# PEER routing in bf16, one gate piece on ScalarE, routings two and four blocks closer

## The chip, the cores and the metric

One core of one Trainium2 chip runs the whole program. The metric is device time in microseconds (us) of one execution. Before the change the median of 3 runs is 3424.29 us (3423.9 to 3427.24).

## What is computed

Two residual layers over 512 tokens of width 1024. Each has an attention mixture, and behind it a PEER layer (product-key experts), which is the stage that the change touches:

```python
def peer(xn, w_q, sub_keys, u, v):
    q = (xt @ w_q).reshape(T, PEER_HEADS, 2, PEER_HALF)
    s = jnp.einsum('thpc,hpnc->thpn', q, sub_keys).astype(jnp.float32)
    s1, i1 = lax.top_k(s[:, :, 0], PEER_TOPK)
    s2, i2 = lax.top_k(s[:, :, 1], PEER_TOPK)
    cand = (s1[..., :, None] + s2[..., None, :])...      # 8 heads x 256 sums
    cidx = (i1[..., :, None] * PEER_N_KEYS + i2[..., None, :])...
    top_s, top_j = lax.top_k(cand, PEER_TOPK)
    expert = jnp.take_along_axis(cidx, top_j, axis=-1)
    gate = jax.nn.softmax(top_s, axis=-1)
    # per token: out = sum over 128 experts of gate * gelu(x . u[expert]) * v[expert]
```

There are 16384 experts (128 x 128), and each token takes 8 heads x 16 of them.

## The kernel before

**Tiling.** The 512 tokens are four tiles of 128 (t = 0 to 3). Tile 0 is done sparsely: GpSimd fetches its experts' rows of u and v by indirect DMA (`fetch`), VectorE multiplies and sums them (`use_row`). Tiles 1 to 3 (384 tokens, `SD`) are done densely: TensorE multiplies them with all of u and all of v, and the hiddens are weighted by a gate matrix that is zero but for the chosen experts.

**Blocks.** `peer_stage` is written as one row of blocks n, and each engine has its own loop over them, in program order. Blocks 0 to 15 project the queries (`NQ`), 16 to 143 multiply with u (`FRONT` is 144), and the 128 behind them with v. A block of u is 24 matmuls of 384 columns into `h_ps` (`product`, L1884), since each fp32 operand is split into a high and a low part: ScalarE makes the high part two blocks ahead (`upper(n + 2)`, L1959, 128x1024), and VectorE or GpSimd the low one (`lower(n + 2)`, L2173 or L1850). ScalarE then takes the product through Gelu (`take`, L1973) and SyncE stores it.

**Routing.** For each tile t VectorE runs `route(t)` as a generator in pieces, one for each block from `route_step[t]` on: 18, 26, 61 and 96 (`LIST_END` is 18). The pieces are: sums of candidates and the upper eight (L2064, L2070), their places (L2074), the lower eight and the shifted scores (L2079 to L2084), arithmetic on the places (L2091 to L2104), then the translation of the places to key numbers. For each side s that is 16 `scalar_tensor_tensor` (L2110: is_equal with c, times key number c) into a table of 16 x 128 fp32, and one `tensor_reduce` over it (L2115). The last piece divides the gates (L2122) and signals `routed`. In the nine blocks of a routing (`ROUTE_PIECES`, `in_route`) GpSimd makes the low part of block n + 2 in VectorE's place, so VectorE's first own low part is that of block `route_step + 11`. VectorE also uses about nine fetched rows in ten blocks throughout (L2181).

**Turning and cutting.** At the end of block `route_step + 9` TensorE waits for `routed` and transposes both picks and the gates into `t_ps` (L1906 to L1908). At `route_step + 10` VectorE cuts the gates into three bf16 pieces (`cut_gates`, L2136 to L2144).

**Gate matrix.** From `route_step + 11` on, 16 batches of 8 tokens follow for each tile, 7 blocks for five batches (`hot_step`). For each, VectorE writes in bf16 `same` (L2160), `rows` (L2164) and three `cols`, one for each piece (L2168), all 128x1024. Two blocks later TensorE multiplies them in the middle of a block (`place_gates`, 24 matmuls, L1920), and ScalarE moves the result (`move_gates`, 2 x 128x512, L1995). Every fourth batch, SyncE stores 2 MB of gates. Four blocks behind the last batch (`WEIGH0`, block 134) SyncE loads the first hiddens and gates back (`load_w`, L1824 and L1825); the first weighings and high and low parts of the weights follow at `WEIGH0 + 3` to `WEIGH0 + 6`. They are needed at block 144.

## Time and profile before

| | |
|---|---|
| median of 3 runs | 3424.29 us |
| profiled execution | 3423.7 us |
| its span, first to last instruction | 3421.9 us |
| mean granted TensorE clock | 0.977 |
| TensorE matmul / VectorE / ScalarE / GpSimd busy | 95% / 78% / 41% / 32% |
| u phase of layer 0's PEER, with the queries | 336 to 1070 us |
| u phase of layer 1's PEER, with the queries | 2144 to 2879 us |

Each engine runs its own program in order and waits on semaphores. In the views below "x16" means that many instructions merged into one row, "[5.96 <-DVE ...]" means that the engine sat idle for 5.96 us until that instruction of VectorE (DVE) ended, and PE, ACT, POOL and SP are TensorE, ScalarE, GpSimd and SyncE. Layer 0's tiles are called p0r_..., layer 1's p1r_....

### The profile page before, as it was taken

How to read it: one execution, taken by the hardware profiler on the slowest of the kernel's cores; microseconds unless marked ns; L12 is line 12 of the kernel's file. 1: busy time of each engine (PE TensorE's matmuls, PEld its weight loads, DVE VectorE, ACT ScalarE, POOL GpSimd, SP SyncE). 2: the span in 40 equal slices, each digit the busy share in tenths (PEclk: the TensorE clock that was granted, in tenths of full speed). 3: DMA queues.
4: the chain of work that ended last, by engine and by line, in shares of the span. 5: the costliest groups of instructions: out<-in, count | busy, mean ns of one | idle time of the engine just before them, and what ended most of it. 6: DMA issues, size and time to landing. Idle time of an engine off the chain costs nothing. (4 is left out here: it accounts for less than half of the span.)

```text
span 3421.9 us, 49213 instructions
## 1 busy us (share of the span) xinstructions
PE 3255.3 (95%) x18534; PEld 2913.3 (85%) x18534; DVE 2667.6 (78%) x5415; ACT 1400.2 (41%) x2205; POOL 1098.5 (32%) x666
## 2 busy tenths in 40 slices
PE   7988999999999999998999997999999999999997
PEld 6866899999998888886978876899989998888886
DVE  4664799888976889885367875799898976888886
ACT  3333245544453333333345544235545453333332
POOL 1311363333422465550000001354242422455451
PEclk9998999999999999999999999999999999999999
DMA  4102358878889999994122212348778789999994
GB/s 164 62 7 89 127 163 288 297 268 294 274 310 352 406 392 402 387 397 144 71 80 69 75 44 81 130 138 293 288 268 282 271 313 350 409 398 394 392 396 178
DMA packets 324348, 833.65 MB, mean 244 GB/s; under 512 B 26000, under 2 KB 160656, under 8 KB 320016
## 3 DMA queue, kind: packets, MB, share of 16 engines
q1 hardware_dynamic: 250384, 562.04, 45.8%
q0 software_dynamic: 73728, 268.47, 21.3%
q8 instruction: 148, 2.42, 0.3%
q14 instruction: 88, 0.72, 0.1%
HBM read 721.30 MB, written 109.10 MB: 243 GB/s over the span
## 5 line engine op out<-in xcount | busy, mean ns | idle before, releaser
L1959 ACT ACTIVATE peer_hi<-peer_raw 128x1024 fp32r<-128x1024 f32 x540 | 570.7, 1057 | 648.8 <-PE p_bank L1933 501.1
L2173 DVE TENSOR_TENSOR peer_lo<-peer_raw,peer_hi 128x1024 fp32r<-128x1024 f32 x434 | 532.0, 1226 | 315.2 <-ACT peer_hi L1959 314.9
L1862 POOL DMA_INDIRECT p_grow<-in_u_rows,p_expert x256 | 331.2, 1294 | 750.1 <-DVE p_hid L2181 736.1
L1862 POOL DMA_INDIRECT p_grow<-in_v_rows,p_expert x256 | 425.1, 1660 | 372.4 <-DVE p_acc L2190 331.4
L1933 PE MATMUL p_bank<-peer_hi,p_w_hi 128*128 128x512 f32 x1536 | 473.1, 389 | 0.8 <-DVE peer_lo L2173 0.8
L1933 PE MATMUL p_bank<-peer_hi,p_w_lo 128*128 128x512 f32 x1536 | 473.0, 389 | 0.0
L1933 PE MATMUL p_bank<-peer_lo,p_w_hi 128*128 128x512 f32 x1536 | 472.8, 389 | 0.0
L1884 PE MATMUL p0r_h_ps<-peer_x_hi,peer_hi 128*128 128x384 f32 (+1 forms) x1152 | 400.8, 348 | 9.7 <-ACT p_h_sb L1973 5.8
L1884 PE MATMUL p1r_h_ps<-peer_x_hi,peer_hi 128*128 128x384 f32 (+1 forms) x1152 | 401.1, 348 | 9.3 <-ACT p_h_sb L1973 5.6
L1884 PE MATMUL p1r_h_ps<-peer_x_hi,peer_lo 128*128 128x384 f32 (+1 forms) x1152 | 394.9, 343 | 0.0
L1884 PE MATMUL p1r_h_ps<-peer_x_lo,peer_hi 128*128 128x384 f32 (+1 forms) x1152 | 394.9, 343 | 0.0
L1884 PE MATMUL p0r_h_ps<-peer_x_hi,peer_lo 128*128 128x384 f32 (+1 forms) x1152 | 394.8, 343 | 0.0
L1884 PE MATMUL p0r_h_ps<-peer_x_lo,peer_hi 128*128 128x384 f32 (+1 forms) x1152 | 394.7, 343 | 0.0
L1850 POOL TENSOR_TENSOR peer_lo<-peer_raw,peer_hi 128x1024 fp32r<-128x1024 f32 x106 | 267.9, 2529 | 372.7 <-ACT peer_hi L1959 372.1
L1933 PEld LDWEIGHTS p_bank<-peer_hi,p_w_hi 128*128 128x128 f32 x1536 | 288.1, 188 | 61.4 <-DVE peer_lo L2173 1.7
L1933 PEld LDWEIGHTS p_bank<-peer_hi,p_w_lo 128*128 128x128 f32 x1536 | 288.3, 188 | 60.0
L1933 PEld LDWEIGHTS p_bank<-peer_lo,p_w_hi 128*128 128x128 f32 x1536 | 288.3, 188 | 59.8
L2181 DVE CUSTOM_DVE_ANT_0 p_grow<-p_grow,p_xrow 128x1024 f32<-128x1024 f32 x256 | 318.2, 1248 | 0.8
L2190 DVE SCALAR_TENSOR_TENSOR p_acc<-p_grow,p_w,p_acc 128x1024 f32<-128x1024 f32 x252 | 317.6, 1279 | 0.0
L1884 PEld LDWEIGHTS p0r_h_ps<-peer_x_hi,peer_hi 128*128 128x128 f32 x1152 | 218.5, 190 | 15.3 <-issue 9.1
L1884 PEld LDWEIGHTS p1r_h_ps<-peer_x_hi,peer_hi 128*128 128x128 f32 x1152 | 218.6, 190 | 15.0 <-issue 8.6
L1884 PEld LDWEIGHTS p1r_h_ps<-peer_x_lo,peer_hi 128*128 128x128 f32 x1152 | 218.3, 189 | 5.2
(365 smaller groups left out, 5589.2 us busy)
## 6 DMA issues: line engine op xcount, KB each, us to landing
peer_raw<-in_u SPq DMA_DIRECT2D x256, 512.0 KB, 5.0
peer_raw<-in_v SPq DMA_DIRECT2D x256, 512.0 KB, 9.1
hiddens<-p_h_sb SPq DMA_DIRECT2D x256, 192.0 KB, 3.7
p_w_raw<-hiddens SPq DMA_DIRECT2D x64, 768.0 KB, 8.0
p_g_sb<-gates SPq DMA_DIRECT2D x64, 768.0 KB, 11.7
gates<-x SPq DMA_DIRECT2D x12, 2048.0 KB, 9.6
ba_w<-in_w_b_mix SPq DMA_DIRECT2D x38, 512.0 KB, 3.6
peer_raw<-in_w_peer_q SPq DMA_DIRECT2D x32, 512.0 KB, 3.8
```

Source lines behind the costliest of these rows:

```text
L1850: pool.tensor_tensor(lo[:, m % NH, :], raw[:, m % NR, :], hi[:, m % NH, :].bitcast(F32), ALU.subtract).then_inc(lo_pool, 1)
L1862: pool.indirect_dma_start(out=grow[:, g % RG, :], out_offset=None, in_=table, in_offset=bass.IndirectOffsetOnAxis(ap=expert[:, at:at + 1], ...
L1884: mm = pe.matmul(h_ps[:, n % 2, first:S], a[:, n % NH, at], b[:, k, first:S], start=(k == 0 and s == 0), stop=(k == KC - 1 and s == 2))
L1933: mm = pe.matmul(bank[:, t, half, :], w[:, c % 2, b, t * P:(t + 1) * P], v[:, n % NH, half * HALF:(half + 1) * HALF], start=j == 0 and s = ...
L1959: act.activation(hi[:, n % NH, :], raw[:, n % NR, :], ACT.Copy).then_inc(hi_ready, 1)
L2173: dve.tensor_tensor(lo[:, m % NH, :], raw[:, m % NR, :], hi[:, m % NH, :].bitcast(F32), ALU.subtract).then_inc(lo_dve, 1)
L2181: dve.tensor_tensor_reduce(row, row, xrow[:, :], 1.0, 0.0, ALU.mult, ALU.add, hid0[:, at:at + 1]).then_inc(used, 1)
L2190: dve.scalar_tensor_tensor(out=acc[:, at % 2, :], in0=row, scalar=w0[:, at:at + 1], in1=acc[:, at % 2, :], op0=ALU.mult, op1=ALU.add).then ...
```

## The change

- **Routing in bf16.** The key numbers are copied as bf16 pairs (`best_b`), the places are written as bf16 (`place_b`), and the table `hit` is bf16. For each side: one is_equal over all 2048 elements, 8 multiplications of 256 elements, and, in place of the reduction, a tree of additions over 1024, 512, 256 and 128 elements.
- **Gate columns.** Piece 0 is kept in fp32 (`piece0`, rounded to bf16 through `rounded`). ScalarE makes its columns (`weigh_columns`): 8 activations of 128 elements for each batch, each scaled by a column of `piece0`, one block behind the one-hots, between `upper` and `move_gates`. VectorE makes two columns in place of three. New waits: ScalarE for `equal`, and both VectorE's next `same` and TensorE's `place_gates` for `first_cols`.
- **Steps.** Routings start at 18, 26, 59 and 92. TensorE turns at `route_step + 10` in place of + 9, VectorE cuts at + 11 in place of + 10, in the same block as the first one-hots. `WEIGH0` thereby goes from 134 to 130, and the first weighings stand at `WEIGH0 + 6` to `+ 9` in place of `+ 3` to `+ 6`: block 136 in place of 137.

```diff
-    route_step = [LIST_END, LIST_END + 8, LIST_END + 43, LIST_END + 78]
+    route_step = [LIST_END, LIST_END + 8, LIST_END + 41, LIST_END + 74]
...
     def turns_after(t):
-        return route_step[t] + 9
+        return route_step[t] + ROUTE_PIECES + 1
...
     def cut_step(t):
-        return route_step[t] + 10
+        return turns_after(t) + 1
...
-            left = early.sb("left", [P, P])
+            left = index_f
...
                 def place_gates(k):
                     pe.wait_ge(rows_ready, k + 1)
-                    pe.wait_ge(cols_ready, (k + 1) * PIECES)
+                    pe.wait_ge(cols_ready, (k + 1) * (PIECES - 1))
+                    pe.wait_ge(first_cols, k + 1)
...
+                def weigh_columns(k):
+                    if k % TILE_BATCHES == 0:
+                        act.wait_ge(done, k // TILE_BATCHES + 1)
+                    act.wait_ge(equal, k + 1)
+                    if k >= 2:
+
+                        act.wait_ge(multiplied, (k - 1) * BATCH)
+                    for v in range(BATCH):
+                        at = k * BATCH + v
+                        ins = act.activation(cols[:, k % 2, 0, v // 2, :, v % 2], same[:, v // 2, :, v % 2], ACT.Copy,
+                                             scale=piece0[:, at:at + 1])
+                    ins.then_inc(first_cols, 1)
...
+                    if n - 1 in hots_at:
+                        weigh_columns(hots_at[n - 1])
                     if n in place_at:
                         move_gates(place_at[n])
-                    if n == WEIGH0 + 4:
+                    if n == WEIGH0 + 7:
                         upper_w(0)
-                    if n == WEIGH0 + 5:
+                    if n == WEIGH0 + 8:
                         upper_w(1)
...
-                    step.mark(dve.tensor_copy(best_f[:, :, :], best_at[:, t, :, :]))
+                    step.mark(dve.tensor_copy(best_b[:, :, :, :],
+                                              best_at[:, t, :, :].unsqueeze(3).broadcast_to([P, NQ, TOPK, 2])))
...
                     for s in range(2):
-                        place = pos_f[:, 3 * s, :].rearrange("p (h k) -> p h k", k=TOPK)
-                        for c in range(TOPK):
-                            step.mark(dve.scalar_tensor_tensor(
-                                out=hit[:, c, :].rearrange("p (h k) -> p h k", k=TOPK), in0=place, scalar=float(c),
-                                in1=best_f[:, s:NQ:2, c:c + 1].broadcast_to(by_head), op0=ALU.is_equal, op1=ALU.mult))
+                        step(dve.tensor_tensor(hit.rearrange("p c (k b) -> p c k b", b=2),
+                                               place_b[:, s, :].rearrange("p (k b) -> p k b", b=2).unsqueeze(1)
+                                               .broadcast_to(pairs),
+                                               iota2[:, 0:TOPK, :].unsqueeze(2).broadcast_to(pairs), ALU.is_equal))
+                        for a in range(HEADS):
+                            mine = hit[:, :, a * TOPK:(a + 1) * TOPK].rearrange("p c (k b) -> p c k b", b=2)
+                            step.mark(dve.tensor_tensor(
+                                mine, mine, best_b[:, 2 * a + s, :, :].unsqueeze(2).broadcast_to([P, TOPK, TOPK // 2, 2]),
+                                ALU.mult))
                         step.wait()
                         yield
-                        step(dve.tensor_reduce(pick[:, s, :], hit[:, :, :].rearrange("p c k -> p k c"), AX.X, ALU.add))
+                        n = TOPK // 2
+                        while n > 1:
+                            step(dve.tensor_tensor(hit[:, 0:n, :], hit[:, 0:n, :], hit[:, n:2 * n, :], ALU.add))
+                            n //= 2
+                        step(dve.tensor_tensor(pick[:, s, :], hit[:, 0, :], hit[:, 1, :], ALU.add))
...
                     if k:
 
-                        dve.wait_ge(cols_ready, k * PIECES)
+                        dve.wait_ge(cols_ready, k * (PIECES - 1))
+                        dve.wait_ge(first_cols, k)
...
-                    for c in range(PIECES):
-                        dve.tensor_tensor(cols[:, k % 2, c, :, :, :], same[:, :, :, :], per_token(pieces, c, k),
+                    for c in range(PIECES - 1):
+                        dve.tensor_tensor(cols[:, k % 2, c + 1, :, :, :], same[:, :, :, :], per_token(pieces, c, k),
                                           ALU.mult).then_inc(cols_ready, 1)
...
-                    if n == WEIGH0 + 3:
+                    if n == WEIGH0 + 6:
                         weigh(0)
```

## Rows read from the trace of the kernel before

**Rows 1.** The page's first part: busy time, share and instructions of each engine.

```profile
PE 3255.3 (95%) x18534; PEld 2913.3 (85%) x18534; DVE 2667.6 (78%) x5415; ACT 1400.2 (41%) x2205; POOL 1098.5 (32%) x666
```

**Rows 2.** TensorE's waits, layer 0's PEER, 336 to 1072 us: total, times, longest.

```profile
PE p0r_t_ps L1906 <- DVE p0r_gate L2122: 13.2, 3, 6.3
PE p0r_h_ps L1884 <- ACT p_h_sb L1973: 5.8, 1, 5.8
...
PE p0r_h_ps L1884 <- POOL peer_lo L1850: 1.1, 1, 1.1
```

**Rows 3.** The same waits in layer 1's PEER, 2144 to 2882 us.

```profile
PE p1r_t_ps L1906 <- DVE p1r_gate L2122: 14.1, 3, 7.3
```

**Rows 4.** Timeline of TensorE around the wait of t = 2: start, duration, [idle <-releaser].

```profile
694.66 0.34 PE L1884 MATMUL p0r_h_ps<-peer_x_lo,peer_hi 128*128 128x384 f32 x1
700.96 0.47 PE L1906 MATMUL p0r_t_ps<-ident,p0r_pick 128*128 128x128 f32 x1 [5.96 <-DVE p0r_gate L2122]
...
702.30 0.52 PE L1884 MATMUL p0r_h_ps<-peer_x_lo,peer_hi 128*128 128x384 f32 x1
```

**Rows 5.** Stretches: us, busy (x) of PE, PEld, DVE, ACT, POOL, then clock, DMA.

```profile
698.00:706.00 8.00, 5.04 (x19) 5.04 (x20) 7.90 (x14) 0.00 (x0) 4.31 (x3) 0.57 0.64 208
727.10:763.50 36.40, 36.40 (x290) 35.61 (x289) 30.87 (x46) 20.56 (x24) 8.14 (x8) 1.00 0.83 295
```

**Rows 6.** Timeline of VectorE through route(2) and behind it.

```profile
650.03 0.29 DVE L2059 CAST p0r_best_f<-p0r_best_at 128x256 f32<-128x256 uint32 x1
...
661.81 2.45 DVE L2084 TENSOR_TENSOR p0r_shifted<-p0r_top 128x128 f32<-128x128 f32 x1
...
672.30 3.31 DVE L2110 SCALAR_TENSOR_TENSOR p0r_table<-p0r_pos_f,p0r_best_f 128x128 f32<-128x128 f32 x16
...
678.86 3.85 DVE L2115 TENSOR_REDUCE p0r_pick<-p0r_table 128x128 f32<-128x2048 f32 x1
682.74 11.34 DVE L2110 SCALAR_TENSOR_TENSOR p0r_table<-p0r_pos_f,p0r_best_f 128x128 f32<-128x128 f32 x16
...
700.61 0.29 DVE L2122 TENSOR_TENSOR p0r_gate<-p0r_gate,p0r_gsum 128x128 f32<-128x128 f32 x1
...
703.11 1.22 DVE L2173 TENSOR_TENSOR peer_lo<-peer_raw,peer_hi 128x1024 fp32r<-128x1024 f32 x1
```

**Rows 7.** Timeline of GpSimd in the same routing.

```profile
673.83 4.02 POOL L1850 TENSOR_TENSOR peer_lo<-peer_raw,peer_hi 128x1024 fp32r<-128x1024 f32 x1 [4.06 <-ACT peer_hi L1959]
...
686.94 4.76 POOL L1850 TENSOR_TENSOR peer_lo<-peer_raw,peer_hi 128x1024 fp32r<-128x1024 f32 x2
```

**Rows 8.** Groups by line of VectorE, 336 to 1072 us.

```profile
L2168 DVE TENSOR_TENSOR p0r_cols<-p0r_same,p0r_pieces 128x1024 bf16<-128x1024 bf16 x144 | 90.6, 683 | 0.0
...
L2115 DVE TENSOR_REDUCE p0r_pick<-p0r_table 128x128 f32<-128x2048 f32 x8 | 30.5, 3816 | 0.2
```

**Rows 9.** Timeline of ScalarE in the dilated stage: scale by a per-partition column.

```profile
1735.53 2.45 ACT L542 ACTIVATE ba_w_hi<-ba_w,gains 128x128 fp32r<-128x128 f32 x8 [4.59 <-PE ba_bank L453]
```

**Rows 10.** Timeline of ScalarE over two blocks, without and with a gate batch.

```profile
626.71 0.49 ACT L1973 ACTIVATE p_h_sb<-p0r_h_ps 128x384 f32<-128x384 f32 x1 [0.69 <-PE p0r_h_ps L1884]
...
630.87 0.49 ACT L1973 ACTIVATE p_h_sb<-p0r_h_ps 128x384 f32<-128x384 f32 x1 [2.72 <-PE p0r_h_ps L1884]
631.26 1.05 ACT L1959 ACTIVATE peer_hi<-peer_raw 128x1024 fp32r<-128x1024 f32 x1
633.66 2.10 ACT L1995 ACTIVATE p0r_gbuf<-p0r_gate_ps 128x512 f32<-128x512 f32 x2 [1.35 <-PE p0r_gate_ps L1920]
636.49 0.49 ACT L1973 ACTIVATE p_h_sb<-p0r_h_ps 128x384 f32<-128x384 f32 x1 [0.72 <-PE p0r_h_ps L1884]
```

**Rows 11.** Groups by line of ScalarE, whole run: 512 elements, strided and plain target.

```profile
L1995 ACT ACTIVATE p0r_gbuf<-p0r_gate_ps 128x512 f32<-128x512 f32 x48 | 50.2, 1157 | 32.6 <-PE p0r_gate_ps L1920 32.6
...
L1967 ACT ACTIVATE p0r_qT<-p0r_h_ps 128x512 f32<-128x512 f32 x16 | 9.6, 598 | 78.3 <-PE p0r_h_ps L1884 78.3
```

**Rows 12.** SyncE's issue queue after the gates' last store.

```profile
1031.64 5.94 SPq L1809 DMA_DIRECT2D hiddens<-p_h_sb  x1
```

More of the change, by code:

```diff
@@ L1665, in turns_after @@
     def turns_after(t):
-        return route_step[t] + 9
+        return route_step[t] + ROUTE_PIECES + 1
     def cut_step(t):
-        return route_step[t] + 10
+        return turns_after(t) + 1
     def hot_step(k):
-        return route_step[1 + k // TILE_BATCHES] + 11 + (k % TILE_BATCHES) * 7 // 5
+        return cut_step(1 + k // TILE_BATCHES) + (k % TILE_BATCHES) * 7 // 5
     def place_block(k):
@@ L1728, in peer_stage @@
             places = early.sb("places", [P, 2, SD], BF16)
-            pieces = early.sb("pieces", [P, PIECES, SD], BF16)
+            piece0 = early.sb("piece0", [P, SD])
+            rounded = early.sb("rounded", [P, P], BF16)
+            pieces = early.sb("pieces", [P, PIECES - 1, SD], BF16)
             qT = early.sb("qT", [P, 2, S])
@@ L1734, in peer_stage @@
             rest = early.sb("rest", [P, TT, NK])
-            best_f = early.sb("best_f", [P, NQ, TOPK])
-            table = early.sb("table", [P, TOPK * HK])
+            best_b = early.sb("best_b", [P, NQ, TOPK, 2], BF16)
+            place_b = early.sb("place_b", [P, 2, HK], BF16)
+            table = early.sb("table", [P, 2 * HEADS * CANDS])
             cand, crest = [table[:, i * HEADS * CANDS:(i + 1) * HEADS * CANDS].rearrange("p (h c) -> p h c", c=CANDS)
                            for i in range(2)]
-            hit = table[:, :].rearrange("p (c k) -> p c k", k=HK)
+            hit = table[:, 0:TOPK * HK // 2].bitcast(BF16).rearrange("p (c k) -> p c k", k=HK)
             top = early.sb("top", [P, HEADS, TOPK])
@@ L1771, in peer_stage @@
          cut, done, equal, rows_ready, cols_ready, multiplied, g_moved, weighted, w_hi_ready, w_lo_ready, x_loaded,
-         xrow_ready, indexed, used, hidden, weighed, added, gain_loaded, x_stored) = [st.sem(s) for s in (
+         xrow_ready, indexed, used, hidden, weighed, added, gain_loaded, x_stored, first_cols) = [st.sem(s) for s in (
              "hi_ready", "lo_pool", "lo_dve", "summed", "taken", "keys_loaded", "scored", "listed", "own", "shift_done",
@@ L2101, in route @@
                     step(dve.tensor_tensor(pos_f[:, 1, :], pos_f[:, 1, :], flat_f[:, :], ALU.mult))
-                    step.mark(dve.tensor_tensor(pos_f[:, 0, :], pos_f[:, 0, :], pos_f[:, 1, :], ALU.add))
+                    step.mark(dve.tensor_tensor(place_b[:, 0, :], pos_f[:, 0, :], pos_f[:, 1, :], ALU.add))
                     step(dve.tensor_tensor(pos_f[:, 2, :], pos_f[:, 2, :], flat_f[:, :], ALU.mult))
-                    step(dve.tensor_tensor(pos_f[:, 3, :], pos_f[:, 3, :], pos_f[:, 2, :], ALU.add))
+                    step(dve.tensor_tensor(place_b[:, 1, :], pos_f[:, 3, :], pos_f[:, 2, :], ALU.add))
@@ L2105, in route @@
                     yield
                     by_head = [P, HEADS, TOPK]
+                    pairs = [P, TOPK, HK // 2, 2]
                     for s in range(2):
[L2108 to L2112 removed]
+                        step(dve.tensor_tensor(hit.rearrange("p c (k b) -> p c k b", b=2),
[7 more added lines that the diff above has]
+                                ALU.mult))
@@ L2135, in cut_gates @@
                     at, gates = slice((t - 1) * P, t * P), t_ps[:, 2 * P:3 * P]
-                    dve.tensor_copy(pieces[:, 0, at], gates).then_inc(cut, 1)
+                    before = (t - 1) * 5
+                    if t > 1:
+                        dve.wait_ge(cut, before)
+                    dve.tensor_copy(rounded[:, :], gates).then_inc(cut, 1)
                     dve.tensor_copy(places[:, :, at], t_ps[:, 0:2 * P].rearrange("p (a b) -> p a b", b=P))\
                         .then_inc(cut, 1)
-                    dve.wait_ge(cut, t * 4 - 2)
-                    dve.tensor_tensor(left[:, :], gates, pieces[:, 0, at], ALU.subtract).then_inc(cut, 1)
-                    dve.wait_ge(cut, t * 4 - 1)
-                    dve.tensor_copy(pieces[:, 1, at], left[:, :]).then_inc(cut, 1)
-                    dve.wait_ge(cut, t * 4)
-                    dve.tensor_tensor(pieces[:, 2, at], left[:, :], pieces[:, 1, at],
+                    dve.wait_ge(cut, before + 2)
+                    dve.tensor_copy(piece0[:, at], rounded[:, :]).then_inc(cut, 1)
+                    dve.tensor_tensor(left[:, :], gates, rounded[:, :], ALU.subtract).then_inc(cut, 1)
+                    dve.wait_ge(cut, before + 4)
+                    dve.tensor_copy(pieces[:, 0, at], left[:, :]).then_inc(cut, 1)
+                    dve.wait_ge(cut, before + 5)
+                    dve.tensor_tensor(pieces[:, 1, at], left[:, :], pieces[:, 0, at],
                                       ALU.subtract).then_inc(done, 1)
```

8 lines of the change are left out of this document (4 added, 4 removed).

## The prediction

> **What bounds the kernel now.** I read the page's busy shares first: TensorE's matmuls fill 95% of the span, the other three have room [rows 1]. So only TensorE's stalls and its clock can be won, and the second view is TensorE's waits in the two u phases. The largest is the turn of a routing: 13.2 us in layer 0 and 14.1 us in layer 1, each over three tiles [rows 2, 3]. The timeline of TensorE gives the middle one of layer 0: the matmul at 694.66 is the last, the transpose starts at 700.96 after 5.96 us of idling for `p0r_gate` L2122, the end of `route(2)`, and behind it the same matmul takes 0.52 us in place of 0.34 [rows 4], with the granted clock at 0.57 over those 8 us (so it fell to 1.2 GHz for most of them) [rows 5]. The other late one of layer 0 is 6.3 us [rows 2], layer 1's longest is 7.3 [rows 3]; the remaining three share what is left: 13.2 - 6.3 - 6.0 = 0.9 for t = 1, and in layer 1 14.1 - 7.3 = 6.8, which I split as in layer 0 into 6.0 and 0.8. Two waits are left besides, for ScalarE's take (5.8) and for GpSimd's low part (1.1) [rows 2]. Where the gate matrix is built TensorE never waits: 36.40 us busy of 36.40, with VectorE at 30.87 and ScalarE at 20.56 [rows 5].
>
> The third view is VectorE through `route(2)`. It starts at 650.03, `p0r_gate` ends at 700.90 [rows 6]: 50.9 us. Sixteen L2110 take 3.31 us for side 0 and 11.34 us for side 1; a lone `shifted` of 128 elements takes 2.45 [rows 6]. GpSimd's timeline explains it: each slow one coincides with a low part on GpSimd (two in a row, 4.76 us, from 686.94; another took 4.02 at 673.83 while VectorE's sixteen ran) [rows 7]. The two shut each other out. The reduction, 3.85 us from 678.86 [rows 6], isn't stretched: in the whole phase its mean is 3816 ns [rows 8].
>
> **The translation, step by step.** Before, per side: 3.31 + 3.85, with gaps 7.2 us, twice 14.4. After: one_hots' bf16 operations take 683 ns for 1024 elements [rows 8]; three of them in the timeline advance by about 0.60 each, so 0.53 for the elements and 0.07 fixed. is_equal over 2048: 1.14; eight of 256: 8 x 0.20 = 1.6; the tree: 0.60, 0.33, 0.20, 0.20 = 1.33; six gaps where a wait follows, at some 0.12: 0.7. Per side 4.8, twice 9.5. Gain 4.9, less 0.3 for the twice as long key copy (0.29 now, row 650.03 [rows 6]): **4.6 us per routing**, if GpSimd costs as much as before. If the pair patterns ran at one element per cycle, the side would cost 1.1 + 1.1 + 1.1 more, and the gain were below zero.
>
> GpSimd still makes nine low parts per routing (`ROUTE_PIECES` is unchanged), each about 2.4 us. Of `route(2)` some 15 us were such blocking: 8.0 on side 1's sixteen and 2.2 on `shifted` [rows 6], the rest on a cast and a used row, which look alike (two rows of that kind, 2.6 and 2.1 over their usual length). That is six low parts at 2.5; the reduction hid a seventh. After, nothing hides it, but the routing starts 2.6 us later against the blocks, so one more lies in the part that isn't blocked (searching for maxima). I take no change, and keep -2.4 to +2.4 us for the range.
>
> The Trainium skill ("SBUF — State Buffer", section "SBUF: two separate sides") says that a GpSimd operation and a VectorE one with two SBUF inputs or in a two-port mode exclude each other for a whole instruction. The trace agrees, with 11.34 against 3.31 us for the same sixteen instructions. The rule speaks against the tree, whose additions have two inputs each where the reduction has one; by it alone the +2.4 would be taken, and the sum would be 10 us worse over four late routings.
>
> **The turn, one block later, and who is late next.** The allowance doesn't grow by a block. A block is 4.16 us, with a gate batch 5.62 (take to take: 626.71, 630.87, 636.49 [rows 10]). Before, `routed` had to come within 10 blocks of 4.16 plus the 1.7 us by which VectorE starts ahead of block 61: 43.3 us, plus 1.4 of another stall at block 66. After, TensorE turns at the end of block `route_step + 10`, but block + 11 is the first whose low part VectorE makes itself, and it stands behind `routed` and two used rows: from 700.90 to 703.11 + 1.22 [rows 6] is 3.4 us. Allowance: 11 x 4.16, plus 1.46 since batch 15 now falls into the routing's second block, minus 0.9 (start behind batch 15's one-hots, an estimate from 1.7 ahead with two spare blocks gone), minus 3.4: 42.9. So **the wait shrinks by 4.6 - 0.4 = 4.2 us** and part of it moves from the transpose to the first product of the block behind. Four late routings: 6.0, 6.3, 6.0, 7.3 become 1.8, 2.1, 1.8, 3.1: **-16.8 us**. For t = 1 two faster routings stand behind each other: the 0.9 and 0.8 go, **-1.7**. The slow matmuls behind a stall cost 0.18 each, at twice the usual spacing, about 1.6 us per late turn [rows 4], 6.5 in all. The waits left are a third to a half as long, and whether they still bring the lower clock no row shows: between 0 and -6.5, nearer to none of it left, so **-5**.
>
> **ScalarE.** Nearest row: eight 128-element activations with a per-partition scale take 2.45 us [rows 9], so 0.29 each, 2.35 per batch. In a block with both a batch to weigh and one to move: 0.39 to the next + 1.05 upper [rows 10] + 2.35 + 2.10 moves = 5.9, less overlaps 0.2, against 5.62; but over seven blocks 7 x 1.4 + 5 x 2.35 + 5 x 2.0 = 31.6 of 36.4. Queued behind the eight are the moves and the next take and upper; TensorE needs the move a block later and the high part two later, 2.4 us and more of cover. If the cover went, each us would be TensorE's. The other end: 512 elements to a strided target take 1157 ns against 598 to a plain one [rows 11], 1.1 ns more per element, which makes 0.43 each. I take 0.29, since a target step of 4 bytes is a plain fp32 step. Cost to TensorE: **0**.
>
> The Trainium skill ("Advanced Engine Details and Errata", section "SBUF Cachelines") has full speed as long as accesses hit the same 16-byte line twice, which a 4-byte step does and L1995's 128-byte step doesn't. No run so far shows it for this pattern; it lowers the chance of the slow case.
>
> **The rest, at nothing.** VectorE's one-hots shrink by one of five, and its next `same` now waits for ScalarE, which ends some 3.9 us into a block where `same` began at 2.8: a loss of about 1.1 against a gain of 0.6, covered by the two blocks by which low parts are early and by 5.5 idle us in 36.4 [rows 5]. `cut_gates` has one cast more (0.3), covered by the two blocks to `place_gates`. First weighings come one block earlier in absolute terms and are due at 144: covered by four blocks. `load_w` and the last gates' store keep their distance (last batch + 4 and + 2), so SyncE's queue should choke alike: a 5.94 us issue of a hiddens store [rows 12] behind which ScalarE's take is late. All DMAs behind move four blocks with it. The 5.8 us wait stays, within +-2; were it to vanish, another 14 us would go.
>
> **Sum.** 3423.7 - 16.8 - 1.7 - 5 = 3400.2 for the profiled execution; it lies 0.6 below the median, so 3401.
>
> **Rivals.**
> - *All four late waits vanish*, if GpSimd's low parts fall where VectorE doesn't want the memory. For it: TensorE's four late waits differ by up to 1.3 us for the same code [rows 2, 3], so the overlap is loose, and 2 us less blocking in each would do. Against: all that is left of the translation has two inputs. 27.3 of waits, 6.5 of clock and 1: 3389. Chance 0.18.
> - *Nothing is gained on the late ones*: bf16 pairs run at half the assumed rate, or each gap in the tree lets GpSimd in, and the new chain `routed`, two rows, low part takes the place of the turn's wait. For it: 11.34 us where it was shut out [rows 6]. Against: 683 ns for 1024 bf16 elements in pairs [rows 8]. Only t = 1's goes: 3422. Chance 0.17.
> - *ScalarE becomes the bound* while the gate matrix is built. It decides from 0.43 us per activation: 7 x 1.4 + 5 x 3.44 + 5 x 2.0 = 37 of 36.4. At 0.50 it is 39.8, 3.4 us lost per five batches, 19 times: +65, less 20 of routings: 3468; at 0.45, +19 - 20: no change. Against: [rows 9]. Slower, chance 0.08.
>
> **How the numbers follow.** The forecast as such (3394 to 3409) has 0.47, and 0.10 lies between it and "nothing" (3409 to 3418). The range takes in both 3389 and 3422 with a little behind each: 3387 to 3424; ScalarE's case, and the choke's vanishing, are left out. About 0.2% (7 us) is what a measurement can tell from no change: below 3417.4 is faster, 0.47 + 0.18 + 0.10 = 0.75; same 0.17; slower 0.08.
>
> **What would show it.** In the trace after: TensorE's waits on `gate` L2122 are 0 to 2 us each, with waits for `peer_lo` L2173 at four first products, 1 to 3 us; route(2) from its first cast to `gate` is 46 us (50.9 before); a tree's four additions take 1.8 us where GpSimd is still; the eight activations take 2.45 us as one row; the take's 5.8 us wait stands four blocks earlier; no waits of TensorE for `cols` or for `x`/`gbuf` L1995. It would be wrong if waits show up in the stretches of the gate matrix, if a routing takes 49 us or more, or if the choke at the weights' load changes size.

## The result and the profile after

Before 3424.29 us, after 3404.48 us (medians; 3399.16 to 3408.79 over five runs). The ratio is 0.9929, 95% interval 0.9918 to 0.994: by it 24 us less, with 4 us of uncertainty (the two medians alone are 20 us apart). "Less" and "more" between two changed kernels are read below from their ratios, each to the kernel before measured beside it. The profiled execution of the changed kernel took 3399.16 us and is its fastest, its span is 3397.3 and its mean granted clock 0.981.

The page's busy times answer [rows 1]: VectorE has 73 us less, ScalarE 210 us more, and TensorE 7 us less for the same number of matmuls.

```profile
PE 3248.7 (96%) x18534; PEld 2906.7 (86%) x18534; DVE 2594.4 (76%) x5261; ACT 1610.1 (47%) x2973; POOL 1081.4 (32%) x666
```

TensorE's waits of the whole run (total, times, longest) answer [rows 2, 3]. No wait on a routing's `gate` is left. What is left waits for ScalarE's take or for VectorE's low part: 22.8 us in sum. Before it was 40.9: 27.3 for the turns, 11.4 for the take and 2.2 for GpSimd's low part.

```profile
PE p1r_h_ps L1887 <- ACT p_h_sb L1977: 10.5, 4, 7.0
PE p0r_h_ps L1887 <- ACT p_h_sb L1977: 7.6, 3, 4.8
...
PE p0r_h_ps L1887 <- DVE peer_lo L2208: 2.7, 2, 1.4
...
PE p1r_h_ps L1887 <- DVE peer_lo L2208: 2.0, 2, 1.3
```

The same waits as rows of TensorE's timeline in layer 0: t = 1, t = 2, two in the middle of t = 3's routing, and the one at the first weight loads.

```profile
528.97 0.45 PE L1887 MATMUL p0r_h_ps<-peer_x_hi,peer_hi 128*128 128x384 f32 x1 [1.30 <-DVE peer_lo L2208]
...
691.87 0.45 PE L1887 MATMUL p0r_h_ps<-peer_x_hi,peer_hi 128*128 128x384 f32 x1 [1.37 <-DVE peer_lo L2208]
...
837.41 0.41 PE L1887 MATMUL p0r_h_ps<-peer_x_hi,peer_hi 128*128 128x384 f32 x1 [1.27 <-ACT p_h_sb L1977]
...
843.35 0.41 PE L1887 MATMUL p0r_h_ps<-peer_x_hi,peer_hi 128*128 128x384 f32 x1 [1.54 <-ACT p_h_sb L1977]
...
1013.52 0.66 PE L1887 MATMUL p0r_h_ps<-peer_x_hi,peer_hi 128*128 128x384 f32 x1 [4.77 <-ACT p_h_sb L1977]
```

Stretches (us, busy of PE, PEld, DVE, ACT, POOL, granted clock, DMA), to be held against [rows 5]. Around t = 2's turn the clock is 1.00 where it was 0.57; at the weight loads it is still 0.81; and where the gate matrix is built TensorE is as full as before, with VectorE at 26.44 us (30.87) and ScalarE at 31.21 (20.56).

```profile
690.00:698.00 8.00, 6.63 (x39) 6.38 (x38) 7.86 (x16) 2.99 (x5) 6.37 (x4) 1.00 1.00 353
...
1004.00:1022.00 18.00, 13.23 (x61) 12.94 (x60) 7.02 (x9) 5.36 (x7) 3.55 (x3) 0.81 0.96 338
725.00:761.40 36.40, 36.40 (x289) 35.61 (x289) 26.44 (x38) 31.21 (x64) 7.85 (x6) 1.00 0.82 290
```

VectorE's timeline through `route(2)` answers [rows 6]: 643.26 to 688.39, 45.1 us where it was 50.9. A set of eight multiplications shut out by GpSimd takes 3.77 us, the three additions of a tree 1.47 us when nothing is in the way and 3.94 when something is.

```profile
643.26 0.42 DVE L2078 CAST p0r_best_b<-p0r_best_at 128x512 bf16<-128x512 uint32 x1
...
665.72 1.21 DVE L2129 TENSOR_TENSOR p0r_table<-p0r_place_b,iota 128x2048 bf16<-128x2048 bf16 x1
666.97 3.77 DVE L2135 TENSOR_TENSOR p0r_table<-p0r_table,p0r_best_b 128x256 bf16<-128x256 bf16 x8
...
671.93 1.47 DVE L2142 TENSOR_TENSOR p0r_table<-p0r_table 128x1024 bf16<-128x1024 bf16 x3
673.43 0.29 DVE L2144 TENSOR_TENSOR p0r_pick<-p0r_table 128x128 f32<-128x128 bf16 x1
...
682.09 3.94 DVE L2142 TENSOR_TENSOR p0r_table<-p0r_table 128x1024 bf16<-128x1024 bf16 x3
...
688.10 0.29 DVE L2151 TENSOR_TENSOR p0r_gate<-p0r_gate,p0r_gsum 128x128 f32<-128x128 f32 x1
...
690.59 1.22 DVE L2208 TENSOR_TENSOR peer_lo<-peer_raw,peer_hi 128x1024 fp32r<-128x1024 f32 x1
```

Where the 24 us are: from the first product of the first block to that of the last (143), layer 0 took 729.4 us before and 717.2 after, layer 1 730.6 and 719.1. That is 12.2 and 11.5 us, and within 1 us all of the difference between the two profiled executions.

### The profile page after: what moved, and what is told of

It reads as the page before. It is cut to its first block and busy times, and to the rows that moved or that the text cites. A ratio compares the mean times of both kernels' runs of the same rounds, so it can differ in the third digit from the quotient of the medians.

```text
span 3397.3 us, 50111 instructions
## 1 busy us (share of the span) xinstructions
PE 3248.7 (96%) x18534; PEld 2906.7 (86%) x18534; DVE 2594.4 (76%) x5261; ACT 1610.1 (47%) x2973; POOL 1081.4 (32%) x666
## 5 line engine op out<-in xcount | busy, mean ns | idle before, releaser
L1865 POOL DMA_INDIRECT p_grow<-in_v_rows,p_expert x256 | 411.3, 1607 | 387.1 <-DVE p_acc L2225 344.2
L1887 PEld LDWEIGHTS p0r_h_ps<-peer_x_lo,peer_hi 128*128 128x128 f32 x1152 | 217.6, 189 | 5.2
```

The source lines that it names most:

```text
L1865: pool.indirect_dma_start(out=grow[:, g % RG, :], out_offset=None, in_=table, in_offset=bass.IndirectOffsetOnAxis(ap=expert[:, at:at + 1], ...
L1887: mm = pe.matmul(h_ps[:, n % 2, first:S], a[:, n % NH, at], b[:, k, first:S], start=(k == 0 and s == 0), stop=(k == KC - 1 and s == 2))
```

## The experiments

The change has four parts that can be separated: the bf16 translation, the first gate piece on ScalarE, the turn one block later, and the closer starts. Six kernels do one alone or undo one, two change a detail of the new code, and four try the waits that are left. The turns of t = 2 and 3 are called the late turns, and an instruction of VectorE that stands still beside a low part of GpSimd is called shut out or caught. `route(2)` of layer 0 is read in each kernel as two pieces, up to the first comparison of the translation (search) and from there to `gate` (translation), with the number of GpSimd's low parts that start in the translation:

| kernel | search + translation (us) | low parts in the translation |
|---|---|---|
| before | 22.3 + 28.6 | 5 |
| before_close: fp32, closer | 26.1 + 23.7 | 3 |
| after_fp32: fp32, closer | 20.1 + 25.5 | 4 |
| before_bf16: bf16, old starts | 22.3 + 26.2 | 5 |
| after_wide: bf16, old starts | 22.3 + 26.7 | 5 |
| after | 22.5 + 22.7 | 4 |
| after_halves: bf16, closer | 22.4 + 20.9 | 3 |
| after_reduce: reduction, closer | 22.5 + 25.6 | 4 |

### The turn alone (before_turn)

```
-        return route_step[t] + 9
+        return route_step[t] + 10
...
-        return route_step[t] + 10
+        return route_step[t] + 11
```

> The kernel before with one thing changed: the turn at route_step + 10 and the cut at + 11, each one block later. Theory (chain): behind the end of a routing stand two used rows and VectorE's low part of block route_step + 11, 3.4 us, and TensorE needs that low part at the end of the same block + 10. So the four late waits only change their name: about 2 us for gate at the turn and some 3.3 us for peer_lo behind it, together 5.3 in place of 6.0; 3420 us. Rival (a whole block is won): waits of about 1.8, 2.1, 1.8 and 3.1 us and no clock drop, 3424 - 17 - 6 = 3401 us.

Measured: 3428.19 us against 3427.24, ratio 1.0 [0.999, 1.001]. The late waits change their name, and of their sum more than two thirds stay (12.3 us before and 9.1 here in layer 0); a late turn of layer 0 now costs 2.9 us at `peer_lo` and up to 2.0 at `gate`:

```profile
PE p0r_h_ps L1884 <- DVE peer_lo L2173: 5.8, 2, 2.9
...
PE p0r_t_ps L1906 <- DVE p0r_gate L2122: 3.3, 2, 2.0
```

So the chain `routed`, two used rows, low part stands right behind the turn, as the prediction has it: a later turn alone gives nothing that the times can tell (between the first and the last block of the profiled executions it is 1.1 and 1.7 us).

### ScalarE's gate columns alone (before_cols)

The kernel before with `weigh_columns` and the pieces of the change (`index_f` shares `flat_f`'s place, for want of room).

> The kernel before with the columns of piece 0 on ScalarE alone (two small buffers share memory with others, so that it fits). Theory: TensorE never waits while the gate matrix is built, so nothing is gained: 3422 to 3427 us, with VectorE some 55 us less busy and ScalarE some 235 us more. Rival (VectorE's load there sets when a routing can begin): the routings start over 1 us earlier against the blocks and waits for gate shrink as much, 3418 us. Rival (ScalarE becomes the bound): above 3431 us with waits for cols or moves.

Measured: 3429.07 us, ratio 1.0004 [0.9994, 1.0014], the routings at 50.9 and 50.7 us. By itself this part is free and useless; the runs on the timetable below show that it isn't so in company.

### The bf16 translation alone (before_bf16)

```
-                    step.mark(dve.tensor_copy(best_f[:, :, :], best_at[:, t, :, :]))
+                    step.mark(dve.tensor_copy(best_b[:, :, :, :],
+                                              best_at[:, t, :, :].unsqueeze(3).broadcast_to([P, NQ, TOPK, 2])))
...
```

> The kernel before with the translation of the places in bf16 alone (pairs, 8 multiplications, tree of additions); steps, turn and gate columns as before. Theory: the late routings (50.9, 49.7, 50.9, 50.7 us from the first cast to the gate) shorten by 3 to 6 us, and as nothing else is touched TensorE's waits for gate (6.0, 6.3, 6.0, 7.3) shorten by the same: about 3402 us. Rival (all of it came from the steps): routings within 1.5 us of before, 3420 us or more.

Measured: 3428.67 us, ratio 1.0 [0.999, 1.001]. The forecast of some 20 us for this part was wrong.

```profile
PE p1r_t_ps L1907 <- DVE p1r_gate L2133: 13.5, 3, 5.6
PE p0r_t_ps L1907 <- DVE p0r_gate L2133: 12.5, 3, 5.1
```

`route(2)` is 2.4 us shorter and its wait 0.9 (5.96 to 5.04), since a stall of 1.4 us at block 66, which had given it time, is gone too; the four late waits are 0.4 to 1.8 us shorter. That of t = 1 grew from 0.88 to 2.36 in both layers: `route(1)` is 2.0 us shorter but starts 3.5 us later, behind a longer `route(0)`. There the translation takes 21.1 us in place of 19.7, and the cast of the experts behind it 2.4 in place of 0.2; in the changed kernel, which does the same there, VectorE's rows are

```profile
471.04 3.55 DVE L2142 TENSOR_TENSOR p0r_table<-p0r_table 128x1024 bf16<-128x1024 bf16 x3
...
474.95 3.34 DVE L2129 TENSOR_TENSOR p0r_table<-p0r_place_b,iota 128x2048 bf16<-128x2048 bf16 x1
...
487.38 2.39 DVE L2158 CAST p_expert<-p0r_index_f 128x128 uint32<-128x128 f32 x1
```

Three steps that take 1.47, 1.21 and 0.23 us when they are alone sit behind a low part each (GpSimd's start at 470.66, 474.82 and 487.30). The reduction that the tree replaces lay there unhindered: 3.90 us at 471.39 in the kernel before. (Putting it back doesn't shorten `route(0)` again, see after_reduce.)

### The timetable alone (before_close)

```
-    route_step = [LIST_END, LIST_END + 8, LIST_END + 43, LIST_END + 78]
+    route_step = [LIST_END, LIST_END + 8, LIST_END + 41, LIST_END + 74]
...
```

with the turn and the cut of before_turn.

> The kernel before with only the timetable changed: routings two start at +41 and +74 instead of +43 and +78, the turns and the cut one block later; the fp32 translation, VectorE's three gate columns and the weighings stay. Theory (the timetable carries most of the gain, since the closer start lays the routing differently against GpSimd's low parts and ScalarE's takes): routing lengths of core 0 near those of the run with the fp32 translation, 45.5 and 49.5 us in place of 50.9 and 49.7, the waits on the third piece of the route near 2.5 us in sum, and the time 3410 +- 4. Rival (the timetable needs the lighter columns, because VectorE comes to the routing later with three columns of each batch than with two): routings stay at 50 us or more, waits of 5 us and more before the turns of t=2 and t=3, and the time 3420 to 3430.

Measured: 3418.99 us against 3429.28, ratio 0.9964 [0.9949, 0.9978]: 12 us, between the two expectations. The routings are 49.7 and 48.6 us. Two rows show why `route(2)` gains so little here. Its first additions and GpSimd's first low part:

```profile
644.28 3.36 DVE L2064 TENSOR_TENSOR p0r_table<-p0r_best 128x512 f32<-128x512 f32 x2
```

```profile
644.45 2.77 POOL L1850 TENSOR_TENSOR peer_lo<-peer_raw,peer_hi 128x1024 fp32r<-128x1024 f32 x1 [22.31 <-ACT peer_hi L1959]
```

In after_fp32, where VectorE has one operation of five less in the gate batch just ahead, the routing starts 0.6 us earlier in its block: the two additions run from 643.01 and take 1.15 us, and the low part starts only at 643.77.

### All but the bf16 translation (after_fp32)

The changed kernel with the translation of before (`index_f` again shares `flat_f`'s place).

> The changed kernel with the fp32 translation of before (16 scalar_tensor_tensor and a reduction per side; one small buffer shares memory so that it fits). Theory: routings are 3 to 5 us longer again, and TensorE's waits at blocks route_step + 10 and + 11 grow from at most 1.4 to 4 to 6 us at t = 2 and 3, with the lower clock behind them: 3399 + 4 x 4 + 4 = 3419 us. Rival (closer steps and the later turn carry the gain): within 4 us of the changed kernel, 3403 us.

Measured: 3410.21 us, ratio 0.994 [0.9916, 0.9963], so 21 of the 24 us without bf16. That the closer steps change no length was wrong: `route(2)` takes 45.5 us, close to the changed kernel's 45.1, but only since its search is 2.4 us shorter; its translation is 2.8 us longer. `route(3)` takes 49.5 where the changed kernel has 47.4.

Held against before_close, which differs from it by the gate columns (and by the first weighings, three blocks earlier), this run also shows what ScalarE's columns are worth in company: 21 us of gain in place of 12. The routing that starts 0.6 us earlier in its block is 4 us shorter (45.5 for 49.7), and the wait of t = 2 is 1.24 us where before_close has 2.79 and 2.53. The intervals of the two runs overlap a little; from the first to the last block the layers of the profiled executions are 7.0 and 4.7 us shorter. The changed kernel with all three columns on VectorE wasn't run.

### All but the closer starts (after_wide)

`route_step` back to + 43 and + 78.

> The changed kernel with the routings' distance of before (steps 18, 26, 61, 96). What the first four runs left open: with the fp32 translation the closer kernel's routing still took 45.5 us (t = 2), and the bf16 translation alone only shortened it from 50.9 to 48.5. Theory now (where the routing lies against GpSimd's low parts sets its length): routings of t = 2 and 3 go back to 48 to 49 us, TensorE waits 3 to 5 us for peer_lo and gate at each late turn, 3399 + 4 x 4 + clock 4 = 3419 us. Rival (the distance is nothing, the gate columns on ScalarE freed VectorE): routings of 45 to 47 us, at most 3405 us.

Measured: 3419.37 us against 3428.6, ratio 0.998 [0.997, 0.999]: 17 us of the gain are gone with this one line. The routings are 49.0 and 48.4 us, and each late turn of layer 0 costs 2.9 at `peer_lo` and up to 1.5 at `gate`:

```profile
PE p0r_h_ps L1887 <- DVE peer_lo L2208: 7.1, 3, 2.9
...
PE p0r_t_ps L1909 <- DVE p0r_gate L2151: 2.3, 2, 1.5
```

What follows from the table and these runs: at the same number of low parts in it, the bf16 translation is 2.8, 2.8 and about 2.1 us shorter (3, 4 and 5 of them), not 4.6; and each low part that lies in the translation costs 1.8 to 4 us, while one that lies in the search may cost next to nothing (22.3 us with four, 22.5 with five). after_pool10 below adds a low part to the same routing at the same start: its translation grows from 22.7 to 25.6 us, 2.9 for that one. The number alone doesn't set the length, though: a search with five takes 20.1, 22.5 or (in `route(3)`) 24.4 us. What each falls on matters too, as the two rows of before_close show for one. The closer start moves one low part from the translation of `route(2)` to its search and shortens it by 3.9 us (3.1 in layer 1, from 48.5 to 45.4). The 5.8 us of `route(2)` are 2 to 3 of arithmetic and 3 to 4 of that.

### The tree against a reduction (after_reduce)

```
-                        n = TOPK // 2
-                        while n > 1:
...
+                        step(dve.tensor_reduce(pick[:, s, :], hit.rearrange("p c k -> p k c"), AX.X, ALU.add))
```

> The changed kernel with the tree of additions replaced by one tensor_reduce over the bf16 table. Unhindered the tree costs 1.8 us a side and the reduction 3.8, so 4 us more per routing. Theory (a reduction isn't shut out by GpSimd's low parts, the tree is): it hides one or two low parts of 2.2 us, so the routings of t = 2 and 3 are 44.5 to 47.5 us (45.1 and 47.4 with the tree), routing 0 is shorter than 39.6, and the time is within 3 us of the changed kernel. Rival (only unhindered costs count): routings 4 us longer, 49 and 51, and 3415 us.

Measured: 3435.86 us against 3428.6, ratio 1.0021 [1.001, 1.0033]: 31 us slower than the change, with the bf16 comparisons kept. The eight reductions of layer 0 (a group of VectorE's: busy, mean ns) don't care about GpSimd, and are as slow as over fp32:

```profile
L2140 DVE TENSOR_REDUCE p0r_pick<-p0r_table 128x128 f32<-128x2048 bf16 x8 | 30.9, 3864 | 0.1
```

A tree shut out once costs up to 3.94 + 0.29, hardly more than the reduction; one that isn't, 1.76. In each of the changed kernel's four late routings one of the two trees is shut out. The routings of t = 1, 2, 3 are 2.0, 3.0 and 3.2 us longer (37.8, 48.1, 50.6), and all six turns wait again: 8.6 us at `peer_lo` and 2.7 at `gate` in each layer. Some 8 us of routing in a layer cost 12 to 14 us between its first and last block. The rival was right on the lengths, though the time lies 20 us above its 3415; the theory was wrong. The shorter `route(0)` that it expected didn't come either: 39.6 us with the tree, 39.7 with the reduction, since now its first eight multiplications take 5.98 us in place of 3.78, and the cast behind it is caught as before.

### One more low part on GpSimd (after_pool10)

```
-    in_route = {s + i for s in route_step for i in range(ROUTE_PIECES)}
+    in_route = {s + i for s in route_step for i in range(ROUTE_PIECES + 1)}
```

> The changed kernel with one low part more per routing on GpSimd: block route_step + 11, the one that stands behind the end of the routing on VectorE. Theory (chain): TensorE's waits for VectorE's peer_lo (1.3, 1.4, 1.3, 0.7 us) go, and the gate is early enough at the turn; 3 to 6 us less than the changed kernel, 3394 us. Rival (the tenth low part shuts VectorE out for 2.4 us more, and the gate itself is late at the turn): waits for gate of 1 to 2 us in their place, 3399 to 3402 us.

Measured: 3409.86 us against 3428.6, ratio 0.994 [0.9923, 0.9957]. The theory's gain didn't come. The waits on `peer_lo` are gone as meant, but the tenth low part lengthens `route(2)` to 48.1 us, and others come:

```profile
PE p1r_t_ps L1909 <- DVE p1r_gate L2151: 2.3, 2, 1.8
PE p1r_gate_ps L1924 <- ACT p1r_cols L1997: 1.6, 2, 0.8
PE p0r_gate_ps L1924 <- ACT p0r_cols L1997: 1.6, 2, 0.8
```

### The exponentials one block later (after_exp7)

In t = 3's routing ScalarE idles 7.07 us for the store of the hidden values of two blocks earlier, and then meets the exponentials, whose two table loads cost 1.28 us each (its timeline in the changed kernel):

```profile
836.78 0.49 ACT L1977 ACTIVATE p_h_sb<-p0r_h_ps 128x384 f32<-128x384 f32 x1 [7.07 <-DMA hiddens<-p_h_sb]
838.72 1.06 ACT L1963 ACTIVATE peer_hi<-peer_raw 128x1024 fp32r<-128x1024 f32 x1 [1.45 <-DMA peer_raw<-in_u]
839.80 1.28 ACT L1981 ACT_TABLE_LOAD   x1
```

```
-        return route_step[t] + 6
+        return route_step[t] + 7
```

> The changed kernel with ScalarE's exp of the gates (and its two table loads, 2.6 us) at route_step + 7 in place of + 6. Theory: at t = 3 it stood behind a take that was late for its hiddens' store, and TensorE's waits for ScalarE at blocks 98 and 99 (1.3 + 1.5 us in layer 0, 3.5 in layer 1) come from the two together. One block later the exp finds ScalarE on time: the second of these waits goes in each layer, 3 to 5 us in all, 3395 us. Rival (the store alone makes the waits): they stay, 3399 us, and the gate may come later.

Measured: 3405.21 us, ratio 0.993 [0.9912, 0.9948], no gain. In layer 0 the two waits for the take (1.27 and 1.54 us) become one of 1.95, with one of 1.44 for GpSimd's low part behind it, and the waits for VectorE's low parts grow from 2.7 to 3.4. ScalarE still idles 7.4 us for the store. So the exponentials alone don't make these waits.

### ScalarE's operations in halves (after_halves)

```
-                        ins = act.activation(cols[:, k % 2, 0, v // 2, :, v % 2], same[:, v // 2, :, v % 2], ACT.Copy,
-                                             scale=piece0[:, at:at + 1])
+                        for part in (slice(0, NK // 2), slice(NK // 2, NK)):
+                            ins = act.activation(cols[:, k % 2, 0, v // 2, part, v % 2], same[:, v // 2, part, v % 2],
+                                                 ACT.Copy, scale=piece0[:, at:at + 1])
```

> The changed kernel, with each of ScalarE's gate column operations cut in two of 64 elements, so 16 in place of 8 for a batch: 48 batches in a layer, and 16 more fixed costs. Theory (ScalarE has little room at the gate batches: 20.6 of 36.4 us without the columns; the columns are 8 at 0.31 us of issue each): the eight more cost about 1.6 to 2.4 us a batch, ScalarE's takes come late by that at batches that lie one block apart, and TensorE waits for the take or for the columns, 5 to 60 us in all: 3410 to 3465. Rival (ScalarE's room covers even the doubled number, as it covered the single one): no wait of TensorE's for columns or moves, the time 3404 within 4.

Measured: 3453.64 us against 3429.28, ratio 1.0072 [1.0056, 1.0089]: 49 us slower than the change. The columns of a batch, in the changed kernel and here:

```profile
722.86 2.48 ACT L1997 ACTIVATE p0r_cols<-p0r_same,p0r_piece 128x128 bf16<-128x128 bf16 x8
```

```profile
563.46 3.95 ACT L1998 ACTIVATE p0r_cols<-p0r_same,p0r_piece 128x64 bf16<-128x64 bf16 x16
```

1.5 us more a batch, and TensorE waits for the moves:

```profile
PE p0r_gate_ps L1924 <- ACT x L2013: 7.2, 8, 1.0
...
PE p0r_gate_ps L1924 <- ACT p0r_gbuf L2013: 2.9, 3, 1.0
```

So the room that ScalarE has in the stretch with the gate batches (5.2 us of 36.4, by the row at 725.00) is real and small: it covers the columns, and not 1.6 times their cost, which over the five batches there is 7.3 us more. Seven blocks with five batches now take 37.86 us in place of 36.42, and ScalarE is busy in all of them:

```profile
727.00:764.86 37.86, 36.88 (x292) 35.70 (x290) 28.46 (x41) 37.86 (x105) 10.28 (x7) 1.00 0.83 287
```

That is 27 us for the 96 batches. The profiled execution lost 45 between the first and last blocks of the two layers; the other 18 lie at the late turns. VectorE's next `same` waits 35.3 us for the columns in layer 0 here (18.2 in the changed kernel, where it costs TensorE nothing), so VectorE reaches `route(2)` 4.5 us later in its block, and TensorE then waits 2.9 us at `peer_lo` though the routing itself is 1.7 us shorter.

### The second weight load three blocks later (after_loads)

```
                     if n == WEIGH0:
                         load_w(0)
+                    if n == WEIGH0 + 3:
                         load_w(1)
```

> The changed kernel, with the second of the two first weight loads issued three blocks later than the first instead of right behind it. Theory (the late take at block 133 waits because SyncE's issues stand behind two large loads at once): ScalarE's late take there, 4.8 and 7.0 us of TensorE's waits, falls to under 2 us on both profiled cores and the slow clock behind it goes: 3404 less 5 of the wait and less 5 of the clock, 3394 (3390 to 3399). Rival (the queue is choked by the weight traffic as such, whatever the two issues' distance): the wait of 5 to 7 us stands at the same block or three blocks on, 3404.

Measured: 3393.22 us against 3429.28, ratio 0.9886 [0.9869, 0.9903], beside 0.9929 [0.9918, 0.994] for the change alone: the largest gain of a single edit here. SyncE's issues in the changed kernel (start, us) answer [rows 12]; a load and a store choke in one go for 8 us, and ScalarE's take needs that store:

```profile
998.96 4.55 SPq L1827 DMA_DIRECT2D p_w_raw<-hiddens  x1
1003.55 0.53 SPq L1828 DMA_DIRECT2D p_g_sb<-gates  x1
1004.13 3.49 SPq L1812 DMA_DIRECT2D hiddens<-p_h_sb  x1
```

and with the loads apart, two of 3 us, each short enough for the buffers:

```profile
1003.55 3.26 SPq L1812 DMA_DIRECT2D hiddens<-p_h_sb  x1
...
1014.65 2.91 SPq L1812 DMA_DIRECT2D hiddens<-p_h_sb  x1
```

TensorE's wait of 4.8 us becomes two of 0.9 and 0.4; the one of 7.0 in layer 1 becomes 1.8. From the first to the last block the layers take 711.5 and 711.6 us, 5.7 and 7.5 less than in the changed kernel. New behind it is one wait of 3.8 us for a low part in the v phase (0.5 in the changed kernel), so it isn't yet the end of what this place holds.

### A third buffer for the hidden values (after_ring)

```
-        h_sb = st.sb("h_sb", [P, 2, SD])
+        h_sb = st.sb("h_sb", [P, 3, SD])
```

on top of after_loads; the first pieces lie in the keys' place to make room.

> The changed kernel with the second first weight load three blocks later, as in the run before, and a third buffer for the hidden values that ScalarE takes and SyncE stores (it lies where the keys were, together with the first gate pieces). Theory (ScalarE's takes at block 98 and at blocks 131 to 134 come late because the store of two blocks earlier, issued behind the 2 MB store of gates at 820.90, has not landed, and there are only two buffers): with a third one the late takes go, TensorE's waits for the take fall from 4.7 and 4.2 us in the two layers to under 1.5 us each, with the slow stretches behind them: 3393 less 8, so 3385 (3380 to 3389). Rival (the transfers themselves are late, and the raw blocks that ScalarE's upper parts and VectorE's low parts need lie behind the same store, so TensorE waits next for the lower parts): the waits for the take change name and keep 3 us or more a layer, 3393 within 3.

Measured: 3390.91 us against 3428.97, ratio 0.9886 [0.9862, 0.9911], not distinguishable from after_loads. At the weight loads no wait for the take is left in either layer, but in t = 3's routing one of 3.9 us (3.0 in layer 1) takes the place of two (1.3 and 1.5 us, and 0.8 and 0.9). There the take is in time, at 833.34, and the high part behind it isn't:

```profile
840.92 1.06 ACT L1964 ACTIVATE peer_hi<-peer_raw 128x1024 fp32r<-128x1024 f32 x1 [7.09 <-DMA peer_raw<-in_u]
```

SyncE issued the 2 MB store of gates at 822.22 and the loads of blocks behind it. It is the transfers that are late, by 7 us, and not a buffer too few: the rival was right for this place, and on the time. That the store is what delays them wasn't tried by moving it.

## Why the prediction was right, and where it wasn't

**The time.** 3401.0 was forecast, with 3387 to 3424; it is 3404.5. The terms for the waits and the clock add up well: -16.8, -1.7 and -5 are -23.5, and the stretches between the blocks give -12.2 and -11.5. Part of that agreement is luck. The waits at the turns shrank by 22.6 us (27.3 to 4.7) where 18.5 were forecast, and GpSimd's 2.2 went too; the waits for the take, forecast to stay, grew by 6.7 (11.4 to 18.1). Together that is -18.1 of waits, and -5.7 for the rest. Inside the first term two errors cancel as well:

**The translation was mis-sized, and the start's place was booked at nothing.** The sum had 4.6 us per routing from bf16, with GpSimd's share unchanged. before_bf16 gives 2.4 and 1.3 us for the late routings of layer 0 (51.1 - 48.5 = 2.6 and 2.4 against before_turn's lengths), and no time at all; with equal numbers of low parts it is 2.1 to 2.8. The missing part came from the closer start, through the low part that falls into the search in place of the translation. The prediction had this as its range of -2.4 to +2.4 us and took the middle; for `route(2)` it is 3 to 4 us, outside that range. For `route(3)` the search got 1.6 us longer and the translation 2.6 shorter than in after_wide, so it gives 1 us. Lengths of 46 us were forecast; they are 45.1 and 47.4.

**What the reduction hid.** It was named, and its return then set off against a shift of phase that isn't there in `route(0)`, whose start the change doesn't move. That routing grew by 1.3 us, the cast behind it by 2.2, and the wait of t = 1, forecast to go, is 1.30 us in both layers in place of 0.88. This term of -1.7 was wrong, by 2.5 us. That the missing reduction is the reason isn't shown: in after_reduce it is back, and `route(0)` and the cast are as long as with the tree.

**The new chain held, the allowance nearly.** For t = 2 the routing is 5.8 us shorter and the wait 4.6 (5.96 to 1.37), so the allowance shrank by 1.2 and not by 0.4: the prediction left the 1.4 us of the stall at block 66 out of the difference, and in layer 0 that stall is gone. The wait has the name that was forecast, `peer_lo` at the first product, as in before_turn. Late waits of 1.8, 2.1, 1.8 and 3.1 us were expected. At the turn they are 1.37 and 0.71 for t = 2 in the two layers, and none for t = 3. Ahead of t = 3's turn stand two waits for ScalarE's take instead, 2.8 and 2.6 us, which weren't foreseen and give its routing time. Their cause is open. The closer start puts the exponentials on the block whose take is late anyway, where before the two lay apart and TensorE didn't wait; but after_exp7 moves them a block on, and 3.4 and 2.2 us of waiting stay. The take itself idles longer for the store, 7.1 us in place of 5.8.

**The clock.** -5 was near the 5.7 us that the waits don't account for, and the traces now show the price. From first product to first product the two blocks of t = 2's turn took 16.8 us before and 10.3 after; two blocks with a turn and no wait take 8.7 (t = 3's in the changed kernel). That is 8.2 us for a wait of 5.96 and 1.6 for 1.37, with after_wide's 6.1 for 4.3 between them: 1.4 us for each us of a long wait and 1.2 for a short one. The granted clock stayed at 1.00 with waits of 1.4 us, and was 0.94 over 30 us around after_wide's. By the same reading the four late turns lost 9.0 us beyond their waits before (6.5 was the forecast's figure) and 0.5 after. That is 8.5 back where 5.7 are left in the whole, so some 3 us were lost again elsewhere; at which of the new waits the traces weren't read.

**ScalarE.** Eight columns in 2.48 us (2.45 from the nearest row), 31.21 us of load in the stretch where the sum had 31.6, no wait of TensorE: right. The prediction cited the Trainium skill, "Advanced Engine Details and Errata", section "SBUF Cachelines", for the 4-byte step; the trace agrees, at 0.29 us from one to the next. after_halves puts the other side on record: at 3.95 a batch the load sum gives 7 x 1.4 + 5 x 3.95 + 5 x 2.0 = 39.6 us, 3.2 lost on each of 19 fives or 60 us. ScalarE took 37.86 for them, 1.4 lost on each or 27 us; what else was lost came at the late turns, through VectorE. It was the right rival, with a price in this stretch more than twice too high. (The prediction's own line for 0.45 us was also off: 37.8 of 36.4, nineteen times, is +27 and not +19.)

**The rule on the shared port.** The prediction weighed the Trainium skill, "SBUF — State Buffer", section "SBUF: two separate sides", against the tree, and put its result at 10 us worse. The traces agree with the rule as such: additions with two inputs are shut out (3.94 us against 1.47), the reduction never (3864 ns in the mean of eight). Its sum is wrong: after_reduce shows the tree 3 to 4 us per late routing better, since only one tree of two meets a low part there.

**The choke at the weight loads** stayed, four blocks earlier: 4.8 and 7.0 us where 5.8 and 5.6 stood, within the +-2. The prediction took it as given; after_loads shows that it was worth 11 to 15 us, about half of the change, and one line.

**Of the rivals**, "nothing on the late ones" is what each part brings alone (before_turn, before_cols, before_bf16), and the sum of parts doesn't add: 0, 0 and 0 for those three, 12 us for the timetable with the turn (before_close), 21 with ScalarE's columns too (after_fp32), 24 for all; and 7 without the closer starts (after_wide). All of them act on one chain with one deadline. By how much bf16 helps in company (3404.5 against 3410.2 us) the intervals don't settle; the 2.1 us of `route(3)` speak for it.

## What to carry to other kernels

Where two engines shut each other out of memory, look at which instructions the other's fall on, and not only at how many there are: the cheaper arithmetic was worth 2 to 3 us per routing here, and a start 2.4 us later against the blocks another 3 to 4 us in `route(2)`, but 1 us in `route(3)`. Parts that shorten one chain towards a fixed deadline must be judged together, since each alone may measure as nothing. And look along the issue queue for large transfers issued back to back: pulling two of them apart gave more than the bf16 arithmetic did.

## What the runs showed of the hardware

- A reduction on VectorE over 2048 elements takes 3.8 to 3.9 us, over bf16 (3864 ns) as over fp32 (3816 ns, [rows 8]), beside GpSimd or not. Additions of two bf16 tensors, 1792 elements in three instructions, take 1.47 us alone and 3.5 to 3.9 us beside one low part of GpSimd (once, in layer 1 of the changed kernel, 6.3 us).
- A short instruction caught behind a low part takes about that part's length: 2.39 us for a cast of 128 elements that takes 0.23 alone, with a low part of 2.39 us started just before it.
- ScalarE's scaled copy of 128 bf16 elements with a target step of 4 bytes follows at 0.29 us; one of 64 elements at 0.25. Most of it is fixed.
- A store of hidden values took 2.9 and 3.3 us to issue behind one pair of weight loads, 3.5 and 5.9 [rows 12] behind two pairs, and ScalarE then waited for its landing; the issue of the second pair's first load took 4.55 us directly behind the first pair and 0.37 us three blocks later.
